# Two transformer blocks on one core: the start of the kernel reordered, norm roots divided between two engines, gate projections of the stick attention re-timed

## The reference

```python
# first block: two layers (a, b)
h = rms_norm(x, a_norm);  q, k, v, qm, gate = split(h @ a_w_in)
q, k = rope(rms_norm(q), cos, sin), rope(rms_norm(k), cos, sin)
o = diff_attention(q, k, v, lam)                 # softmax(q1 k1) - lam * softmax(q2 k2)
o = rms_norm(o, a_subln) * (1 - lambda_init)
om = memory_attention(qm, mem, ...)              # keys and values from rms_norm(mem) @ mem_w_kv
x = x + (concat(o, om) * silu(gate)) @ a_w_out
k_s, v_s = split(rms_norm(x, kv_norm) @ w_kv_shared)
h = rms_norm(x, b_norm);  q, qm, gate = split(h @ b_w_in)
o = stick_breaking_attention(q, k_s, v_s)        # suffix products of sigmoids, no softmax
x = x + (concat(o, memory_attention(qm, mem, ...)) * silu(gate)) @ b_w_out
# second block, twice: three branches (gated MLP, latent attention "mla", gated recurrence)
h = rmsnorm(x, pre); c_q, c_kv, ... = split(h @ w_in)
...  rmsnorm(c_q), rmsnorm(c_kv), latent attention, merge with sigmoid gates
x = x + rmsnorm(merged @ w_out, post)
```

## Time and profile before

| | |
|---|---|
| time before, median of 3 runs (lowest to highest) | 2398.34 us (2397.19 to 2399.38) |
| the profiled execution's own time | 2393.45 us |
| its span, first to last instruction | 2391.4 us |
| granted TensorE clock, mean of the span | 0.977 |
| PE busy / DVE / ACT / POOL | 2234.0 / 1165.1 / 930.7 / 1137.7 us |
| window 0 to 110 us: PE busy, clock | 82.92 us, 0.91 |

### The profile page before, as it was taken

The page is one execution under the profiler, slowest core; times in us unless marked ns, Lnnn a source line. Parts: engine busy times, 40 slices in busy tenths (PEclk is TensorE's granted clock), DMA queues, the critical chain, the costliest instruction groups (busy, mean ns, idle before and its releaser), DMA issues.

```text
span 2391.4 us, 27363 instructions
## 1 busy us (share of the span) xinstructions
PE 2234.0 (93%) x9994; PEld 1697.5 (71%) x9994; DVE 1165.1 (49%) x1813; ACT 930.7 (39%) x1577; POOL 1137.7 (48%) x1364
## 2 busy tenths in 40 slices
PE   6898898998898999999999999889999999999996
PEld 4676566764466666888887788666668888877885
DVE  6787866326736333024319754263330243197543
ACT  3545642345533444232223732334442322237322
POOL 3563225632144323457447575343235574575751
PEclk8999998999999999999999999999999999999998
DMA  3222112321022212233223232212122332232321
GB/s 130 71 88 71 36 53 89 97 71 36 20 78 79 62 53 93 93 97 97 88 88 106 67 110 88 79 62 62 53 88 89 97 97 89 88 106 70 108 87 62
DMA packets 52981, 191.43 MB, mean 80 GB/s; under 512 B 6000, under 2 KB 6256, under 8 KB 52336
## 3 DMA queue, kind: packets, MB, share of 16 engines
q1 hardware_dynamic: 51552, 184.44, 24.7%
q10 hardware_dynamic: 1296, 5.24, 0.6%
HBM read 187.56 MB, written 2.10 MB: 79 GB/s over the span
## 4 chain that ended last, share of the span: by engine, by line
PE 79%; DVE 8%; ACT 6%; POOL 3%; issue 3%; DMA 2%; DVEq 0%; ACTq 0%; SPq 0%
PE proj L518 20%; PE proj L520 20%; PE proj L519 20%; POOL lower L470 3%; PE score L514 3%; PE turned L514 3%; PE stat L514 2%; PE mix L514 2%; PE score L519 2%; PE score L518 2%; PE score L520 2%; PE proj L514 2%; PE ptp L739 1%; DMA raw_ring<-stream 1%; DVE small L1589 1%
## 5 line engine op out<-in xcount | busy, mean ns | idle before, releaser
L470 POOL TENSOR_TENSOR lower<-raw_ring,upper 128x256 fp32r<-128x256 f32 x1360 | 1137.5, 869 | 1210.3 <-ACT upper L1074 1209.9
L518 PE MATMUL proj<-h,upper 128*128 128x512 f32 x1496 | 609.6, 407 | 17.1 <-DVE yf L1732 7.6
L520 PE MATMUL proj<-h,lower 128*128 128x512 f32 x1496 | 586.5, 392 | 0.0
L519 PE MATMUL proj<-h,upper 128*128 128x512 f32 x1496 | 586.0, 392 | 0.0
L1074 ACT ACTIVATE upper<-raw_ring 128x1024 fp32r<-128x1024 f32 x340 | 355.8, 1057 | 560.2 <-PE proj L518 362.5
L518 PEld LDWEIGHTS proj<-h,upper 128*128 128x128 f32 x1496 | 283.8, 190 | 81.5 <-issue 11.5
L520 PEld LDWEIGHTS proj<-h,lower 128*128 128x128 f32 x1496 | 282.6, 189 | 61.1
L519 PEld LDWEIGHTS proj<-h,upper 128*128 128x128 f32 x1496 | 283.7, 190 | 56.7 <-issue 4.3
L518 PE MATMUL proj<-y,upper 128*128 128x512 f32 x628 | 254.7, 406 | 9.2 <-ACT yf L1151 3.5
L520 PE MATMUL proj<-y,lower 128*128 128x512 f32 x628 | 249.8, 398 | 0.0
L519 PE MATMUL proj<-y,upper 128*128 128x512 f32 x628 | 249.7, 398 | 0.0
(11 more groups left out here) (378 smaller groups left out, 3259.0 us busy)
## 6 DMA issues: line engine op xcount, KB each, us to landing
raw_ring<-stream SPq DMA_DIRECT2D x340, 512.0 KB, 3.5
x<-x_in SPq DMA_DIRECT2D x4, 512.0 KB, 6.9
rows<-rows_in ACTq DMA_DIRECT2D x2, 1024.0 KB, 5.3
out<-x SPq DMA_DIRECT2D x8, 256.0 KB, 2.0
memraw<-mem_in SPq DMA_DIRECT2D x1, 1024.0 KB, 11.5
memraw<-mem_in ACTq DMA_DIRECT2D x1, 1024.0 KB, 4.9
rot<-tables_in ACTq DMA_DIRECT2D x2, 512.0 KB, 3.6
ws<-ws_in ACTq DMA_DIRECT2D x2, 256.0 KB, 5.6
```

The lines of the kernel that those rows point to most:

```text
L470: ins = nc.gpsimd.tensor_tensor(lower[:, p % RING, a:b], raw_ring[:, p % RAWS, a:b], upper[:, p % RING, a:b].bitcast(FP32), ALU.subtract)
L518: first_ = nc.tensor.matmul(o, lhsT[0], rhs[0], start=start, stop=False)
L519: nc.tensor.matmul(o, lhsT[0], rhs[1], start=False, stop=False)
L520: return first_, nc.tensor.matmul(o, lhsT[1], rhs[0], start=False, stop=stop)
```

## The change

- The stream's first five slots are loaded straight into the memory of `lower` (`landing`), all of them behind x and without a wait; ACT converts from there and the subtraction is done in place. The slots after them use `raw_ring` as before. The subtraction of slot 0 is DVE's (`EARLY = 1`), in one instruction of 1024 columns; POOL begins with slot 1.
- The constants are loaded in two parts: ones, frequencies and signs first, then the positions, and the other constants behind the memory.
- ACT squares x into a place of its own (`x_sq`) and so waits for no sum. DVE adds the squares in pairs, PE sums four pairs instead of eight tiles. ACT converts two slots ahead of the root and three behind it. The memory's squares (`mem_sq`) are summed by PE in one go behind the first `group`, and their root is the first thing in head 1's place.
- DVE computes the angles first, with the pair sums put in between, then slot 0's subtraction, then the norm of x. The natural-log table is loaded right after the sines.
- `group` gets `behind`: the first one takes its fourth slot up only behind input tile 1 and catches up there.
- Roots with `alone`: ACT leaves the Identity out and DVE computes the same value from `stat` after the logarithm, beside ACT's exponential. These are the norms of x, of the latents, and the post norm. Heads, memory and the differential attention's tiles keep the Identity; of two memory heads the second uses the other half of `half_var`.
- `diff_finish`: ACT also squares the estimate; DVE scales `mix` first, and then applies the Newton factor: three instructions where there were four.
- In block b the copies of b.k4 and b.k5 come ahead of the conversion of slots, which follows each.
- The maxima of the memory attention are 2 steps ahead where they were 3; the latent attention keeps 3.
- Stick gates: a gate's eight units end at z = 7, 15, 23, 31, 39 and 44, where they ended at 6, 14, 21, 29, 36 and 44.

```diff
+N_EARLY = CONST_COLS["ident"]
+EARLY = 1
...
+    def slot_source(p):
+        return landing[:, p, :] if p < RING else raw_ring[:, (p - RING) % RAWS, :]
+    def slot_arrival(p):
+        return (landed[p], 16) if p < RING else (arrived[(p - RING) % RAWS], 16 * ((p - RING) // RAWS + 1))
+    def slot_ready(p):
+        return first.after("early_lower", p) if p < EARLY else (split_lower, p + 1 - EARLY)
...
-            return min(z + 1 + (z >= 3) + (z >= 19) + (z >= 35), 8 * MT)
+            return min(z + 1 + min(max(z - 39, 0), 3), 8 * MT)
...
-        sp.dma_start(const[:, :], const_in[:, 0:N_KEPT]).then_inc(consts_loaded, 16)
+        sp.dma_start(const[:, 0:N_EARLY], const_in[:, 0:N_EARLY]).then_inc(consts_loaded, 16)
+        sp.dma_start(pos[:, :].bitcast(INT32), pos_in[0:1, :].partition_broadcast(P)).then_inc(pos_loaded, 16)
         sp.dma_start(fcol[:, :], first_in).then_inc(consts_loaded, 16)
         for n in range(4):
             sp.dma_start(x[:, 2 * n:2 * n + 2, :], x_in[:, 2 * n:2 * n + 2, :]).then_inc(x_loaded[n], 16)
-        for p in range(RAWS):
-            sp.dma_start(raw_ring[:, p, :], stream[p, :, :]).then_inc(arrived[p], 16)
+        for p in range(RING):
+            sp.dma_start(slot_source(p), stream[p, :, :]).then_inc(landed[p], 16)
         sp.dma_start(memraw[:, :, :], mem_in).then_inc(mem_loaded, 16)
-        sp.dma_start(pos[:, :].bitcast(INT32), pos_in[0:1, :].partition_broadcast(P)).then_inc(late_consts, 16)
+        sp.dma_start(const[:, N_EARLY:N_KEPT], const_in[:, N_EARLY:N_KEPT]).then_inc(late_consts, 16)
         sp.dma_start(gate[:, 0, 0:3 * P], const_in[:, N_KEPT:N_CONST]).then_inc(late_consts, 16)
         sp.dma_start(lcols[:, :, :], layer_in).then_inc(late_consts, 16)
-        for p in range(RAWS, SLOTS):
-            sp.wait_ge(split_lower, p + 1 - RAWS)
-            sp.dma_start(raw_ring[:, p % RAWS, :], stream[p, :, :]).then_inc(arrived[p % RAWS], 16)
+        for p in range(RING, SLOTS):
+            if p >= RING + RAWS:
+                sp.wait_ge(*slot_ready(p - RAWS))
+            sp.dma_start(slot_source(p), stream[p, :, :]).then_inc(arrived[(p - RING) % RAWS], 16)
...
-        for p in range(SLOTS):
+        for p in range(EARLY, SLOTS):
...
-        def group(S, C, W, slots, src, key):
+        def group(S, C, W, slots, src, key, behind=0):
...
+            ahead = len(slots) - behind
+            def term(b, k, w, v, start=False, stop=False):
+                return mm(token_bank(j0 + b, b)[:, :], W.slot(slots[b])(k * P, k * P + P)[w], src[:, k, v, :], start, stop)
+            for b in range(ahead):
+                W.need(slots[b])
...
+                begun = term(b, 0, 0, 0, True)
+                term(b, 0, 1, 0)
                 if b == 0:
                     release(W, begun)
...
+            for b in range(ahead):
+                term(b, 0, 0, 1)
...
+                pe.wait_ge(*S.after(*key(k)))
+                for b in range(len(slots) if k > 1 else ahead):
+                    begun = term(b, k, 0, 0)
+                    term(b, k, 0, 1)
+                    ins = term(b, k, 1, 0, stop=k == KT - 1)
                     if k == KT - 1:
                         release(W, begun)
-                    if k == KT - 1:
                         ins.then_inc(*S.mark("projected", ("job", C.next("job"))))
                         plans["released", j0 + b] = W.gone
-                        W.finish(name)
+                        W.finish(slots[b])
+                for b in range(ahead, len(slots) if k == 1 else ahead):
+                    W.need(slots[b])
+                    hold(S, j0 + b, b)
+                    for q in range(2):
+                        for w, v in TERMS:
+                            term(b, q, w, v, q == 0 and (w, v) == TERMS[0])
...
-        squares(S, C, c("ones"), KT)
-        squares(S, C, c("ones"), KT, MEM)
+        m = C.next("norm")
+        for i in range(KT // 2):
+            pe.wait_ge(*S.after("x_pair", i))
+            ins = mm(stat[:, :], c("ones"), x_sq[:, 2 * i + 1, :], i == 0, i == KT // 2 - 1)
+        ins.then_inc(*S.mark("summed", ("sums", m)))
+        def memory_squares():
+            m = C.next("norm")
+            pe.wait_ge(*S.after("sums_used", m - 1))
+            for k in range(KT):
+                pe.wait_ge(*S.after("mem_sq", k))
+                ins = mm(stat[:, 0:MEM], c("ones"), mem_sq[:, k, :], k == 0, k == KT - 1)
+            ins.then_inc(*S.mark("summed", ("sums", m)))
+            pe.wait_ge(late_consts, 16 * N_LATE)
...
-                      together=lambda: group(S, C, W, names("a.q", 4), h, hkey))
+                      together=lambda: (group(S, C, W, names("a.q", 4), h, hkey, 1), memory_squares()))
...
-            root(S, C, scale, cols)
-        def root(S, C, scale, cols=SEQ):
+            root(S, C, scale, cols, alone=cols == SEQ)
+        def root(S, C, scale, cols=SEQ, square=None, half=0, alone=False):
...
-            if m:
-                act.wait_ge(*S.after("half_var_used", m - 1))
-            nc.scalar.activation(half_var[:, 0:cols], stat[:, 0:cols], ACT.Identity, bias=small[:, 1:2], scale=-0.5 * scale)\
-                .then_inc(*S.mark("rooted", ("sums_used", m)))
+            if not alone:
+                if m > half:
+                    act.wait_ge(*S.after("half_var_used", m - 1 - half))
+                nc.scalar.activation(half_var[:, half * cols:half * cols + cols], stat[:, 0:cols], ACT.Identity,
+                                     bias=small[:, 1:2], scale=-0.5 * scale).then_inc(*S.mark("rooted", ("sums_used", m)))
             act.wait_ge(*S.after("ln_var", m))
             nc.scalar.activation(std[:, m % 2, 0:cols], std[:, m % 2, 0:cols], ACT.Exp, scale=-0.5)\
                 .then_inc(*S.mark("rooted", ("std", m)))
+            if square is not None:
+                act.wait_ge(*S.after("std", m))
+                nc.scalar.activation(square, std[:, m % 2, 0:cols], ACT.Square).then_inc(*S.mark("rooted", ("std_sq", m)))
...
+                if i == 1 and together:
+                    root(S, C, 1.0 / DM, MEM)
                 if i:
-                    root(S, C, 1.0 / HD, cols)
+                    root(S, C, 1.0 / HD, cols, half=int(cols == MEM and i == 2))
...
-            t = C.next("sq")
-            if t >= 2:
-                act.wait_ge(*S.after("sq_used", t - 2))
-            nc.scalar.activation(sq[:, t % 2, :], x[:, k, :], ACT.Square).then_inc(*S.mark("squared", ("sq", t)))
-        root(S, C, 1.0 / DM)
-        feed(RAWS)
+            nc.scalar.activation(x_sq[:, k, :], x[:, k, :], ACT.Square).then_inc(*S.mark("squared", ("x_sq", k)))
+        feed(2)
+        root(S, C, 1.0 / DM, alone=True)
+        feed(RING)
         act.wait_ge(mem_loaded, 16)
-        squares(S, C, [(memraw[:, k, :], None) for k in range(KT)], 1.0 / DM, MEM)
-        feed(RING)
+        for k in range(KT):
+            nc.scalar.activation(mem_sq[:, k, :], memraw[:, k, :], ACT.Square).then_inc(*S.mark("squared", ("mem_sq", k)))
         act.wait_ge(*S.after("angles"))
         nc.scalar.activation(rot[:, 0, :], rot[:, 0, :], ACT.Sin).then_inc(*S.mark("sines", ("cos",)))
         nc.scalar.activation(rot[:, 1, :], rot[:, 1, :], ACT.Sin).then_inc(*S.mark("sines", ("sin",)))
         loaded[0] = None
+        tables()
...
                 for t in range(MT):
-                    take(S, C, k1[:, t, :], block=t if t < 4 else 0)
+                    take(S, C, k1[:, t, :], block=t if t < 4 else 0, later=t >= 4)
+                    feed(wanted[0])
...
-                    root(S, C, 1.0 / (P * (QR if n == QR - 1 else KVR)))
+                    root(S, C, 1.0 / (P * (QR if n == QR - 1 else KVR)), alone=True)
...
-            root(S, C, 1.0 / DM)
+            root(S, C, 1.0 / DM, alone=True)
...
-        def inverse(S, C, cols=SEQ):
+        def inverse(S, C, cols=SEQ, half=0, alone=None):
             m = C.next("norm")
+            r, w = std[:, m % 2, 0:cols], half_var[:, half * cols:half * cols + cols]
+            if alone is not None:
+                dve.wait_ge(*S.after("ln_var", m))
+                link(S, nc.vector.tensor_scalar(w, stat[:, 0:cols], -0.5 * alone, -0.5 * EPS, ALU.mult, ALU.add), ("sums_used", m))
             dve.wait_ge(*S.after("std", m))
-            r, w = std[:, m % 2, 0:cols], half_var[:, 0:cols]
             link(S, nc.vector.tensor_tensor(w, w, r, ALU.mult))
             link(S, nc.vector.tensor_tensor(w, w, r, ALU.mult))
             link(S, nc.vector.scalar_tensor_tensor(out=r, in0=w, scalar=1.5, in1=r, op0=ALU.add, op1=ALU.mult),
@@ -1494,7 +1548,7 @@
...
-            m, s = inv or inverse(S, C, cols)
+            m, s = inv or inverse(S, C, cols, alone=1.0 / DM)
...
-                    m, s = inverse(S, C, cols)
+                    m, s = inverse(S, C, cols, int(cols == MEM and i == 1))
...
-                    ahead += [(maxima, 2 if kind == "diff" else 3, kind), (weights, 1, kind)]
```

(47 more changed lines are left out.)

43 lines of the change are left out of this document (15 added, 28 removed).

## The result

The changed kernel takes 2364.84 us (median of 4 runs, 2361.77 to 2366.65) where the kernel before took 2397.77 beside it (4 runs, 2396.93 to 2399.38): ratio 0.9861, 95% interval 0.9848 to 0.9874, 33 us less. A second set of 4 runs gave 2365.04 us, ratio 0.9870 (0.9856 to 0.9883). The forecast was 2374, range 2365 to 2388: the sign is right, the gain of 24 us was too small by 9, and the time lies just under the range. The changed kernel's profiled execution took 2365.37 us, close to its median; that of before had been 4.3 under its own.

A forecast was written before the change was run, and what follows sets the result against it. PE, busy 93% of the span, was taken as the bound, leaving its waits and lower clock to win. Terms 2.5 + 4.4 + 3.8 + 3.7 + 2.8 + 6 + 1 = 24.2 us gave 2374, range 2365 to 2388.

The forecast's parts named there:

- the start: Start of the kernel: new load and DVE order brings head 0's logarithm from 60.63 to 58.1, 2.5 us.
- block a to b: Between the blocks: ACT's wait at `half_var` goes, 3.8 us, and PE's wait for the copy of k, 3.7.
- the stick gates: Stick attention: PE's 7.6 us of gate-product waits go, some 1.6 return as transpose waits; 6 us, bounds 2 and 7.6.
- differential attention and maxima: Differential tile ends lose a DVE instruction, 4.4 us; memory attention's maxima two steps ahead, 1 us (bounds +4 and -6).
- the lone roots: Seven roots outside the start: without ACT's Identity the exponential starts 0.4 us earlier each, 2.8 us; at worst 0.
- rival 3: Start: the port makes DVE and POOL exclude each other, DVE 3.4 us late; 20.8 us in all, 2377.5; chance 0.08.
- rival 4: Memory attention: ACT waits for DVE's maximum in 32 steps, up to 0.94 us each; slower, 2405; chance 0.04.
- marks named ahead: Profile signs: transpose waits up by less than 2, lone-root rows within 0.1; wrong if stick-stage `ptp` waits exceed 8.
- Rival 1: Stick-gate waits return at transposes, ACT's square takes up the differential end, start gives nothing: 12 us, 2386; chance 0.18.
- Rival 2: Start worth 7.8 us with pair sums and DVE free of POOL, stick gates 7.6: 31 us, 2367; chance 0.10.

## Why the forecast was right in its mechanisms and short in its sum

By the stages the sum was short by 9: the start by 3.8, block a to b by 2.9, the stick gates by 2.3, differential attention and maxima by 2.1, a stage that it didn't have by 0.5, and the lone roots were 2.3 too high.

- **Start, 2.5 forecast, 6.3 in the stage, the step that failed most.** Three parts. The 60.63 of the earlier trace rows is the earliest of nine such starts (60.6 to 64.1, mean 62.8): x's first square began at 5.38 there and at up to 7.43 elsewhere, and PE's sums of x took 8.95 and up to 10.3. The new order isn't much better shielded (55.8 to 58.0), but I compared a lucky start with an average one: 2.2 us. The group was priced with the low clock of before's head, which it hadn't: 2.1 us, of which other runs of the new start gave 0.5 back. x's logarithm was 0.9 late, mostly because PE's sums took 1.42 each where I took the 0.9 of the earlier trace rows, a row from the upper clock level; that didn't reach tile 1, at 30.5, which is DVE's path. There the forecast's 30.8 holds partly by luck: slot 0's subtraction took 1.63 and not 2.2, against a later beginning.
- **DVE beside POOL.** Both run slower, neither blocks: 1.10 for two inputs, 1.63 for the 1024-column subtraction that took 1.23 alone, 4.28 for POOL's four pieces. By the rule of the Trainium skill weighed in the forecast (SBUF — State Buffer, "Who interferes with whom") one of the two would have blocked the other for its whole instruction, 0.69 + 0.69 = 1.38 by the forecast's estimate. This trace doesn't agree, and rival 3 falls.
- **Differential attention and maxima, 5.4 forecast, 7.5 in the stages.** The three middle tiles took 15.3 to 15.6 us in before's profile and take 14.6 to 14.8, 0.7 to 0.8 less each, as worked out. 1.9 of the 7.5 is busy time. In the differential stage the lower level went from 2.7 us on average to none, which fits 1.3 of it; that this is the cause isn't tested. The maxima alone gave no time, and rival 4 falls.
- **From a to b, 7.5 forecast, 10.4.** The two waits gave 6.4. The other 4.0 is the clock: filling the waits alone gave 3.7. That was the sum's second failing step: a wait was priced at its own length.
- **Stick gates, 6 forecast, 8.3.** The waits gave 5.9 over the whole stage, and 5.1 in the profile with the gates alone. PE's waits in the 48 stick steps of the kernel before, then of that profile:

```profile
PE proj L518 <- DVE yf L1732: 7.6, 5, 1.9
PE ptp L739 <- ACT pt L1206: 4.6, 9, 0.7
PE ptp L739 <- DVE prob L1581: 1.7, 1, 1.7
PE ptp L739 <- DVE prob L1578: 0.6, 3, 0.2
```

```profile
PE ptp L739 <- ACT pt L1206: 4.6, 10, 0.7
PE ptp L739 <- DVE prob L1581: 3.5, 4, 1.7
PE ptp L739 <- DVE prob L1578: 1.1, 4, 0.5
```

7.6 went and 2.3 came back as waits for transposes, at DVE's scans as foreseen, where 1.6 was forecast. The 2.4 of busy time isn't explained: the lower level lasted 5 to 14 us there against 3 to 17 without the edit, 9.1 against 12.3 on average, and half of that difference, what the lower level can cost, is 1.6.

- **Lone roots, 2.8 forecast, 0.5.** Right at three of seven places. At the four others the root itself is 0.4 shorter but the stage isn't; why not wasn't tried.
- Of the marks named ahead two were missed and one that was to mean wrong was met. The waits for transposes in the stick stage rose from 6.9 to 9.3 in the changed kernel, by 2.4 and not by less than 2, and 9.3 is above the 8 that was to mean wrong. That mark was a poor one, since before stood at 6.9 already. At x's first root the two rows start 1.1 us apart, not 0.1, as DVE was still at slot 0's subtraction, and at the two latents' second roots 4.5 and 5.9. **Rival 1** (waits change their names, 12 us) falls by the idle time alone, 16 us less. **Rival 2** (a start worth more and gates of 7.6, 31 us, 2367) came nearest, for reasons other than its own: DVE wasn't free of POOL.
- **The scale.** The sum was taken from the profiled 2393.45 and shifted by 4.9 to the median. Profile against profile the gain was 28 where 24.2 was forecast. The other 5 us are what before's profiled execution was better than its median: its start was 2.2 us shorter than the average and its differential attention 1.3. Its mean granted clock, 0.977, was no higher than usual.
